# Sums over partitions of the modulation vectors: 160 TensorE transposes, or 32x32 block transposes on VectorE and 0/1 products

## The reference

```python
c_silu = jax.nn.silu(c)
mods = jnp.split(c_silu @ ada_w[layer] + ada_b[layer], N_MOD, axis=-1)      # 9 for each of 2 layers
shift, scale = jnp.split(c_silu @ kv_ada_w + kv_ada_b, 2, axis=-1)          # 2 more
...
h = modulate(rms_norm(x, norm_g[layer, 0]), sh, sc)          # h * (1 + sc) + sh
x = x + MACARON_WEIGHT * (1.0 + g)[:, None, :] * swiglu(h, ffn_w_in[layer, 0], ffn_w_out[layer, 0])
```

## Time and profile before

| | us |
|---|---|
| median of 3 runs | 1204.15 |
| the 3 runs | 1204.82, 1203.78, 1204.15 |
| span of the profiled execution (first to last instruction) | 1202.0 |
| TensorE busy (5752 matmuls) | 1186.9 |
| VectorE busy | 799.3 |
| ScalarE busy | 586.4 |
| GpSimd busy | 559.0 |

### The profile page before, as it was taken

How to read it: one execution, slowest core, us unless ns; L and a number is a source line. 1 busy time by engine, 2 the same in 40 slices (tenths; PEclk the granted TensorE clock), 3 DMA queues, 4 the chain that set the end, 5 groups by cost and what they waited for, 6 DMA issues and landing times.

```text
span 1202.0 us, 15430 instructions
## 1 busy us (share of the span) xinstructions
PE 1186.9 (99%) x5752; PEld 976.4 (81%) x5752; DVE 799.3 (66%) x1118; ACT 586.4 (49%) x764; POOL 559.0 (47%) x417
## 2 busy tenths in 40 slices
PE   9999999999999999999999999999999999999998
PEld 6888788788788888788888888888888887888887
DVE  6885468845786787678768666697673675644423
ACT  5566555665643443454434357444352665544440
POOL 1465334565454443545444226664452463445360
PEclk9999999999999999999999999999999999999999
DMA  9976369845798899459888748798874444766650
GB/s 352 361 272 230 106 237 336 282 161 171 240 349 293 288 352 346 158 169 340 297 309 307 275 176 283 243 332 300 305 296 166 149 156 158 262 218 203 210 192 35
DMA packets 183224, 297.92 MB, mean 248 GB/s; under 512 B 8368, under 2 KB 100208, under 8 KB 183152
## 3 DMA queue, kind: packets, MB, share of 16 engines
q1 hardware_dynamic: 177696, 284.82, 68.0%
q10 hardware_dynamic: 5456, 12.13, 2.9%
HBM read 295.84 MB, written 1.08 MB: 247 GB/s over the span
## 4 chain that ended last, share of the span: by engine, by line
PE 88%; DVE 5%; ACT 2%; issue 1%; SPq 1%; DMA 1%; POOL 1%; ACTq 0%; DVEq 0%
PE ps L1831 26%; PE ps L1844 26%; PE ps L1836 26%; PE ps L2097 2%; PE ps L1981 1%; PE ps L1923 1%; PE ps L1858 1%; PE ps L2009 1%; DVE w_lo L1164 1%; PE ps L1997 1%; DMA raw<-w_in 1%; POOL stat L507 1%; PE ps L1969 1%; PE ps L2020 1%; SPq L474 1%
## 5 line engine op out<-in xcount | busy, mean ns | idle before, releaser
L516 POOL TENSOR_TENSOR w_lo<-raw,w_hi 128x512 fp32r<-128x512 f32 x348 | 480.2, 1411 | 442.5 <-ACT w_hi L647 442.5
L647 ACT ACTIVATE w_hi<-raw 128x2048 fp32r<-128x2048 f32 x188 | 354.5, 1910 | 104.0 <-PE ps L1844 69.3
L1831 PE MATMUL ps<-w_hi,h_hi 128*128 128x512 f32 x1120 | 314.0, 402 | 1.1 <-issue 0.8
L1844 PE MATMUL ps<-w_lo,h_hi 128*128 128x512 f32 x1120 | 301.7, 391 | 1.8 <-DVE w_lo L1164 1.4
L1836 PE MATMUL ps<-w_hi,h_lo 128*128 128x512 f32 x1120 | 300.7, 391 | 0.0
L1164 DVE TENSOR_TENSOR w_lo<-raw,w_hi 128x2048 fp32r<-128x2048 f32 x96 | 223.7, 2334 | 110.8 <-ACT w_hi L647 108.7
L1844 PEld LDWEIGHTS ps<-w_lo,h_hi 128*128 128x128 f32 x1120 | 209.5, 188 | 49.3 <-DVE w_lo L1164 4.0
L1836 PEld LDWEIGHTS ps<-w_hi,h_lo 128*128 128x128 f32 x1120 | 210.4, 188 | 45.9 <-DVE h_lo L1225 0.2
L1831 PEld LDWEIGHTS ps<-w_hi,h_hi 128*128 128x128 f32 x1120 | 200.9, 189 | 43.7 <-issue 6.8
L1150 DVE SCALAR_TENSOR_TENSOR ps<-ada_raw,ccol,ps 128x512 f32<-128x512 f32 x240 | 181.1, 754 | 8.8 <-DMA ada_raw<-ada_w 2.0
L920 ACT ACTIVATE a_hi<-ps 128x512 fp32r<-128x512 f32 x44 | 26.4, 599 | 159.8 <-PE ps L2097 159.8
(11 more groups left out here) (198 smaller groups left out, 978.6 us busy)
## 6 DMA issues: line engine op xcount, KB each, us to landing
raw<-ffn_in SPq DMA_DIRECT2D x176, 512.0 KB, 5.7
ada_raw<-ada_w SPq DMA_DIRECT2D x144, 512.0 KB, 7.2
raw<-ffn_out SPq DMA_DIRECT2D x44, 1024.0 KB, 6.6
raw<-w_in SPq DMA_DIRECT2D x31, 1024.0 KB, 8.8
raw<-w_out SPq DMA_DIRECT2D x8, 1024.0 KB, 5.7
ada_raw<-kv_ada_w SPq DMA_DIRECT2D x16, 512.0 KB, 8.6
raw<-w_kv SPq DMA_DIRECT2D x8, 1024.0 KB, 5.6
bias<-na_bias ACTq DMA_DIRECT2D x16, 256.0 KB, 4.5
```

The lines of the kernel that those rows point to most:

```text
L516: ins = pool.tensor_tensor(w_lo[:, u % RAW, piece], raw[:, u % RAW, piece], w_hi[:, u % RING, piece].bitcast(F32), ALU.subtract)
L647: act.activation(w_hi[:, u % RING, :], raw[:, u % RAW, :], ACT.Copy).then_inc(*S.inc("w_hi_ready", u))
L1831: pe.matmul(bank(b), hi[:, k_in_lhs + k, tok], wh[:, k, c * 512:(c + 1) * 512], start=start and k == 0, stop=False)
L1844: ins = pe.matmul(bank(b), hi[:, k_in_lhs + k, tok], wl[:, k, c * 512:(c + 1) * 512], start=False, stop=stop and k == nk - 1)
```

## The change

The 40 groups of four transposes are gone. Right behind the last accumulation of a half, VectorE transposes `ada_acc` (128x512) in blocks of 32x32 into bank 7 (`part_sums`) and sums runs of 32 columns there into 16 columns of `parts`. After that partition 32 a + i, column 16 half + b holds the sum over the 32 partitions of quadrant a of column 32 b + i of that half. What is left is a sum over the four quadrants, and a move of each result to its partition: `fold_sums(n)` on TensorE does both for 2 to 4 vectors together (one in the last of eight groups, `FOLDS`), by four accumulating fp32 products of `fold[:, at:at+128]` (zeros and ones, 128x128) with every fourth column of `parts` (8 moving columns for each vector). `fold` is zeroed by GpSimd at the start and filled from the identity by one reduction on VectorE behind `constants()`. `reduce_vectors(n)` adds the bias for all vectors of the group at once and scales those that have a scaling; the multiplication by one is left out. `ada_acc` has one buffer in place of two, and VectorE no longer waits for TensorE before writing it.

The groups come at step 31 of encoder layer 0 (vectors 0 and 1) and behind units 50, 62, 85, 101, 130, 142 and 173. Nothing is folded in encoder layer 1 or in the pooling stage.

```diff
@@ -47,6 +47,8 @@
 NEG = -1e30
 
 N_VEC = 20
+FOLDS = ((0, 1), (2, 3, 4, 5), (6, 7), (8, 9, 10), (11, 12, 13), (14, 15, 16), (17, 18), (19,))
+QUAD = 32
...
@@ -225,25 +227,19 @@
 
         return ada_after[(2 * v + half) * HALF_SLOTS + HALF_SLOTS - 1]
 
-    HALVES = [(v, half) for v in range(N_VEC) for half in range(2)]
     sum_step, sum_unit, taken = {}, {}, set()
-    for v, half in HALVES:
-        e = half_end(v, half)
+    for n, vecs in enumerate(FOLDS):
+        e = half_end(vecs[-1], 1)
         if e < first["up", 0, 0]:
             layer = int(e >= first["in", 1])
             s = min(s for s in SUM_STEPS if s >= fill_step(e - first["in", layer]) + 2 + (e - first["in", layer] == 8) and (layer, s) not in taken)
             taken.add((layer, s))
-            sum_step[layer, s] = [(v, half)]
+            sum_step[layer, s] = [n]
...
-        sum_unit[v, half] = e
+        sum_unit[n] = e
...
-        ada_acc = sb("ada_acc", [P, 2, 512])
+        ada_acc = sb("ada_acc", [P, 512])
+        parts = sb("parts", [P, 2, 4, D // QUAD])
+        fold = sb("fold", [P, 2 * P - QUAD])
...
+            pool.memset(fold[:], 0.0).then_inc(*S.inc("fold_zeroed"))
...
@@ -1102,35 +1101,56 @@
                 ins.then_inc(*S.inc("dve_chain", n))
                 dve.wait_ge(S.sem("dve_chain"), n + 1)
 
-            def reduce_vector(v, half):
-                dve.wait_ge(*S.at("ada_sumT_done", v, half))
-                b = job_bank["ada", v, half]
-                dve.tensor_reduce(mods[:, v, 4 * half:4 * half + 4], bank(b).rearrange("p (k c) -> p k c", k=4),
-                                  AX.X, ALU.add).then_inc(*S.inc("ada_reduced", v, half))
-                if half == 0:
-                    return
-                dve.wait_ge(*S.at("ada_reduced", v, half))
-                m = mods[:, v, :]
-                link(dve.tensor_tensor(m, m, bcols[:, v, :], ALU.add))
-                i = v if v < 9 else v - 11
...
-                ins.then_inc(*S.inc("mod_ready", v))
-                dve.wait_ge(*S.at("mod_ready", v))
+            def fold_columns():
+
+                dve.wait_ge(*S.at("fold_zeroed"))
+                dve.tensor_reduce(fold[:, P - QUAD:P], ident.rearrange("p (q r) -> p r q", r=QUAD), AX.X,
+                                  ALU.add).then_inc(*S.inc("fold_ready"))
+
+            def part_sums(v, half):
+
+                turned, at = bank(ADA_BANK), half * (512 // QUAD)
+                n = next(n for n, vecs in enumerate(FOLDS) if v in vecs)
+                link(dve.transpose(turned, ada_acc[:]))
+                if n >= 2 and half == 0 and v == FOLDS[n][0]:
+                    dve.wait_ge(*S.at("folded", n - 2))
+                dve.tensor_reduce(parts[:, n % 2, v - FOLDS[n][0], at:at + 512 // QUAD],
+                                  turned.rearrange("p (b r) -> p b r", r=QUAD), AX.X, ALU.add).then_inc(
+                    *S.inc("parts_ready", v, half))
+                dve.wait_ge(*S.at("parts_ready", v, half))
+
+            def reduce_vectors(n):
+                vecs = FOLDS[n]
+                these = slice(vecs[0], vecs[-1] + 1)
+                dve.wait_ge(*S.at("folded", n))
+                b = job_bank["fold", n]
+                dve.tensor_tensor(mods[:, these, :], bank(b)[:, 0:len(vecs) * KC].rearrange("p (v k) -> p v k", k=KC),
+                                  bcols[:, these, :], ALU.add).then_inc(*S.inc("biased", n))
+                dve.wait_ge(*S.at("biased", n))
+                for v in vecs:
+                    m = mods[:, v, :]
+                    i = v if v < 9 else v - 11
...
+                    else:
+                        S.same("mod_ready", (v,), "biased", (n,))
+                        continue
+                    ins.then_inc(*S.inc("mod_made", v))
+                    S.same("mod_ready", (v,), "mod_made", (v,))
+                    dve.wait_ge(*S.at("mod_ready", v))
 
             def ada(j):
                 part, pair = divmod(j, HALF_SLOTS)
@@ -1142,16 +1162,14 @@
                     if k == 0:
                         link(dve.tensor_scalar(acc, src, c, None, ALU.mult))
                         continue
-                    into = acc
-                    if k == KC - 1:
-                        into = ada_acc[:, part % 2, :]
-                        if part >= 2:
-                            dve.wait_ge(*S.at("ada_sumT_done", (part - 2) // 2, part % 2))
+                    into = ada_acc[:] if k == KC - 1 else acc
                     ins = dve.scalar_tensor_tensor(out=into, in0=src, scalar=c, in1=acc, op0=ALU.mult, op1=ALU.add)
                     if i == 0:
                         link(ins)
                 ins.then_inc(*S.inc("ada_used", j))
                 dve.wait_ge(*S.at("ada_used", j))
+                if pair == HALF_SLOTS - 1:
+                    part_sums(*divmod(part, 2))
 
             def lows(upto):
 
...
@@ -1180,10 +1198,9 @@
 
                 while sums_done[0] <= min(upto, NU - 1):
                     u = sums_done[0]
-                    for v, half in HALVES:
-                        e = sum_unit.get((v, half), NU)
-                        if e + 4 == u and up_sum(e) is None and e != first["pool"]:
-                            reduce_vector(v, half)
+                    for n, e in sum_unit.items():
+                        if e + 4 == u and up_sum(e) is None:
+                            reduce_vectors(n)
...
@@ -1450,6 +1467,7 @@
                 if layer == 0:
                     first_norm()
                     constants()
+                    fold_columns()
...
@@ -1603,7 +1621,6 @@
             modulate_half(1, 0)
             norm_mean("f01", 0)
             modulate_half(1, 1)
-            reduce_vector(*in_pool)
...
@@ -1850,19 +1867,24 @@
                 elif t == NT - 1:
                     ins.then_inc(*S.inc("unit_used", u))
 
-            def ada_sum(v, half):
-
-                pe.wait_ge(*S.at("ada_used", (2 * v + half) * HALF_SLOTS + HALF_SLOTS - 1))
-                b = job("ada", (v, half), ("ada_reduced", v, half))
-                for k in range(4):
-                    ins = pe.transpose(bank(b)[:, k * P:(k + 1) * P], ada_acc[:, half, k * P:(k + 1) * P], ident[:])
-                ins.then_inc(*S.inc("ada_sumT_done", v, half))
+            def fold_sums(n):
+
+                vecs = FOLDS[n]
+                pe.wait_ge(*S.at("fold_ready"))
+                pe.wait_ge(*S.at("parts_ready", vecs[-1], 1))
+                b = job("fold", (n,), ("biased", n))
+                for j in range(P // QUAD):
+                    at = P - (j + 1) * QUAD
+                    ins = pe.matmul(bank(b)[:, 0:len(vecs) * KC], fold[:, at:at + P],
+                                    parts[:, n % 2, 0:len(vecs), j::P // QUAD], start=j == 0,
+                                    stop=j == P // QUAD - 1)
+                ins.then_inc(*S.inc("folded", n))
 
             def ada_jobs(u):
 
-                for v, half in HALVES:
-                    if sum_unit.get((v, half)) == u:
-                        ada_sum(v, half)
+                for n, e in sum_unit.items():
+                    if e == u:
+                        fold_sums(n)
 
             def lhs_wait(kinds):
                 for kind in kinds:
...
@@ -2144,7 +2166,6 @@
                     ins.then_inc(*S.inc("acc_done", ("pool",), t))
 
             pool_product(0, acc_use((("pool",), 0), ("x_ready", "f01", 0)), (0, 1, 2, 3))
-            ada_jobs(u)
...
-            last_job[ADA_BANK] = ("ada_used", N_ADA - 2 * HALF_SLOTS - 1)
+            last_job[ADA_BANK] = ("parts_ready", N_VEC - 2, 1)
```

More of the change, by code:

```diff
@@ L255, in up_sum @@
         return None
-    vec_end = [sum_unit.get((v, 1), 0) + 4 for v in range(N_VEC)]
+    vec_end = [sum_unit.get(n, 0) + 4 for n, vecs in enumerate(FOLDS) for _ in vecs]
     with ExitStack() as ctx:
@@ L399, in short_work @@
         def short_work(layer, s):
-            work = [("ada_reduce", half) for half in sum_step.get((layer, s - 1), [])]
+            work = [("ada_reduce", n) for n in sum_step.get((layer, s - 1), [])]
             work += [("diff", h) for h in range(HEADS_DA) if DA_DIFF[h] == s]
@@ L410, in short_work @@
             work += [("da_scores", h) for h in range(HEADS_DA) if DA_SCORES[h] == s]
-            work += [("ada", half) for half in sum_step.get((layer, s), [])]
+            work += [("ada", n) for n in sum_step.get((layer, s), [])]
             return work
@@ new lines, in reduce_vectors @@
+            def reduce_vectors(n):
[9 more added lines that the diff above has]
+                    i = v if v < 9 else v - 11
+                    scale_of = {1: 3, 4: 4, 7: 5} if v < 9 else {1: 6, 4: 7, 7: 8}
+                    if v in (9, 10):
+                        i, scale_of = v - 9, {1: 9}
+                    if i in scale_of:
+                        ins = dve.scalar_tensor_tensor(out=m, in0=m, scalar=1.0, in1=gcols[:, scale_of[i], :],
+                                                       op0=ALU.add, op1=ALU.mult)
```

(23 more changed lines are left out.)

16 lines of the change are left out of this document (1 added, 15 removed).

## The result

The changed kernel takes 1211.74 us (median of 5 runs, 1211.04 to 1211.91), the kernel before 1204.04 us in 5 runs beside it. The ratio is 1.0061, 95% interval 1.0049 to 1.0072: slower by 7.7 us, where 13.4 less was forecast. The profiled execution spans 1210.0 us against 1202.0.

What follows compares the result with a forecast made beforehand. TensorE's list of instructions was taken as the bound. 18.0 - 3.7 - 0.9 + 1.0 - 1.0 = 13.4 us off the 1202.0 us span gives 1188.6, plus 2.15 for the median: 1190.8 us, range 1187 to 1198.5.

Steps and rivals of the forecast that it cites:

- the sum of 14.3 us net: On TensorE: 18.0 us of removed transposes less 3.7 us of added fold products, 14.3 us saved.
- The 4 in 100 given to slower: Rival, chance 0.04: inserted work makes VectorE the bound in the FFN stretches; 1215 us with a transpose of 5 us.
- 40 groups removed: On TensorE: 40 groups of four transposes go, 0.45 us each, 18.0 us gained.
- 8 fold groups: On TensorE: eight groups of four small fp32 products come, about 0.11 us a product, 3.7 us with hand-over.
- end of the FFNs' up products: After the first and second FFN's up products: TensorE newly waits 0.7 and 0.3 us for VectorE, 1.0 in sum.
- encoder places: Difference of heads in encoder layers 0 and 1: slack 2.3 us covers the 1.5 us inserted, no new wait.
- shrunk waits for `w_lo`: TensorE's waits for `w_lo` at 143.18 and 289.81 us shrink by 0.68 and 0.35 us, 1.0 gained.
- groups that make room for a wait: Groups (4, 0) and (9, 0) precede waits on VectorE, so removing them gains nothing: 0.9 us not gained.
- The rival from "TensorE: Matmul & The Clock Gate": Rival, chance 0.02: small fp32 products cost four transposes each, 14 us instead of 3.7; 1201.1 us.
- "No wait" for the heads' difference in layer 0: Encoder layer 0: TensorE takes the difference 2.3 us after it ends, so 1.5 us inserted leaves 0.8 us slack.
- the loads: Rival, chance 0.05: DMA binds from 315 to 435 us and from 770, 6.3 us less gain, 1197 us.
- late transposes: Rival, chance 0.15: VectorE's transpose takes 3.0 us, four tight places wait 7.5 us more than counted, 1198.3 us.

Runs made afterwards that it cites:

- e1: The changed kernel with an unused tile of 128 bytes a partition behind `fold`, putting `x`, `h_hi`, `a_hi` and later tiles back at their old addresses: 1195.94 us.
- g3: e1 with the four fold products of each group issued twice: 1202.11 us.
- f1: The changed kernel with 128 unused bytes a partition ahead of `raw`, so the weights' tiles move, and no pad behind `fold`: 1211.57 us.
- f2: The changed kernel with 128 unused bytes a partition both ahead of `raw` and behind `fold`: 1194.3 us.

## Why the prediction was wrong

The step that failed is in the first part: "this kernel is the length of TensorE's list of instructions. Anything struck from that list is gained". The length also depends on what the untouched ones of the list cost, and the sum of 14.3 us net took that for fixed. The diff shows the three sizes of tiles, and their sum of -128 bytes could have been worked out. A price could not: in the kernel before the two distances, 0 and 192, differ by a nanosecond (227.4 to 229.0 against 228.9 to 229.4). The places are worth 15.8 us, more than the whole gain forecast, and it turns the sign. None of the rivals had it. The 4 in 100 given to slower stood for VectorE as the bound, which did not happen.

The other terms of the sum are judged by e1, which differs from the changed kernel in places alone (1195.94 us, 5.1 above the forecast). Waits and busy times are from its profile:

| step | forecast, us | shown |
|---|---|---|
| 40 groups removed | -18.0 | -17.5, not tried alone: e1's TensorE is busy 10.2 us less, with the fold's 7.3 in it |
| 8 fold groups | +3.7 | +7.3 by the starts; doubling them cost 6.2 (g3) |
| end of the FFNs' up products | +1.0 | +1.3 (0.61 and 0.66, for 0.7 and 0.3) |
| encoder places | 0 | +1.6 (1.2 and 0.4) |
| shrunk waits for `w_lo` | -1.0 | -1.0 (1.4 to 0.4) |
| groups that make room for a wait | +0.9 | +0.5: the pooling's longest wait went from 1.8 to 2.3, as said; the wait for the encoder's gate stayed at 0.4, so that group was gained after all |

- **The fold term** was mis-sized by 3.6 us, by a misread row. In the earlier trace rows the "x16" are records, and L2009 issues eight products in a job (two heads, two halves of the tokens, two of the keys). Each costs 0.22 us, not 0.108. L2180 is read too low in the same way. The number of products in the loop, held against the count in the row, would have told it. The rival from "TensorE: Matmul & The Clock Gate", "Terms", in the Trainium skill, with 14 us, is not borne out either: a plain fp32 product of 8 to 32 columns costs twice a transpose of 128 columns here (0.22 against 0.11 us), not four times. So does one of 128 columns: in e1 four of them at L2043 take 0.88 us from 60.14.
- **VectorE's places.** The pair of FFN ends came as worked out; at the second the slack was less than the 1.2 us read, since TensorE now comes 5.2 us earlier and VectorE's accumulation only 4.9. "No wait" for the heads' difference in layer 0 was right: its transposes start at 79.62 us in e1 without idle time. The failure is that I looked at one kind of encoder place and took the rest as covered: the product at L2043 and the transposes at 243.14 us were not looked at, nor was the load of the bias, which VectorE's own instructions set free. I had named the encoder as where it would be wrong.
- **Right:** the transpose at 0.75 us (0.727), VectorE's busy time, the shrunk waits, no effect of the loads, and the order of size of what the work is worth: e1's 1195.94 lies in the range of 1187 to 1198.5, the changed kernel does not. That e1 lies there is partly luck. The range went so high for late transposes and for the loads, neither of which came; the forecast's own range ended at 1193. The 1174 us given for TensorE's busy time do not follow from 1186.9 - 14.3, which is 1172.6.

What stays open: why the distance of the stationary tile from the moving one matters, and why 192 is nearly as good as 0 while 224 is not. 96 was not tried, nor were places of PSUM or of other engines' tiles, which moved too. 0.5 us of the busy time in e1 has no owner. Why the clock went to its half level behind the pooling's wait in some profiles and not in others is open too: e1 waited 2.27 us there and kept the full level.

## What to carry to other kernels

When a change adds, drops or resizes a tile, work out by how many bytes the tiles behind it move against those ahead, and hold a change's verdict back until it has been run with a pad that puts them back; compare the busy time of groups that the diff doesn't touch first. Take the price of one instruction from a row only after its count has been matched with the loop that issues it. On an engine's path, every place where another engine waits for it has to be looked at, not one of a kind.

## What the hardware showed that was not expected

In this kernel, where 4500 matmuls of 128x512 in split fp32 run one behind another at full clock, their spacing is 227 to 229 ns when the stationary and the moving tile lie a multiple of 256 bytes apart in a partition, 229 to 230 at 192 bytes, and 232 to 234 ns at 32, 64, 128, 160 and 224. That is 2% of the spacing and, for 128 bytes, 15.8 us of 1212. It went with the distance, not the place (f1, f2), and it needs no other engine (1182 to 1190 us). A plain fp32 product of up to 128 columns leaves two records in the trace, each as far from the next as a transpose (0.11 us).
